# Eighteen instead of twenty seven-product tiles in the last feed-forward part, and attention products that lag one item more

## What is computed

```
def block(args):                      # forgetting attention, per block of 128 queries
    s = jnp.einsum('bhqd,bhkd->bhqk', q_i, kf) + c_i[..., :, None] - c[..., None, :]
    s = jnp.where(key_pos[None, :] <= q_pos[:, None], s, -jnp.inf)
    p = jax.nn.softmax(s, axis=-1)
    return jnp.einsum('bhqk,bhkd->bhqd', p, vf)
...
def swiglu(h, w1, w3, w2):            # w1, w3: 1024 x 2816, w2: 2816 x 1024
    return (jax.nn.silu(h @ w1) * (h @ w3)) @ w2
```

## Time and profile before

| what | us |
|---|---|
| median of 3 runs (lowest to highest) | 1707.92 (1707.61 to 1709.17) |
| the profiled execution, its own time | 1708.51 |
| its span, first to last instruction | 1706.7 |
| first block's attention, scores of item 0 to the last product with values | 259.3 to 362.5 |
| products of the twenty tiles, first to last | 1348.6 to 1564.7 |
| down products, first | 1568.25 |

### The profile page before, as it was taken

One profiled execution on the slowest core, in us unless ns is written; L12 is line 12 of the kernel. 1 busy time (PEld: TensorE's weight loads), 2 busy tenths in 40 slices (PEclk: granted clock), 3 DMA queues, 4 the chain that ended last, 5 costly groups with the idle time before them and its releaser, 6 DMA issues. The chain is left out here.

```text
span 1706.7 us, 21205 instructions
## 1 busy us (share of the span) xinstructions
PE 1595.5 (93%) x8576; PEld 1335.1 (78%) x8576; DVE 1056.9 (62%) x1458; ACT 700.4 (41%) x1021; POOL 439.5 (26%) x360
## 2 busy tenths in 40 slices
PE   5999988988999999999799999998899899998996
PEld 5778875766878888788788778887787899998885
DVE  6675547447987486433765543346853699998333
ACT  5644245543533243323632334444444544443222
POOL 0023303320622011100052012223432655553002
PEclk8999999989999899999899999999999999999998
DMA  7242212342254254222426423224443132224211
GB/s 285 99 148 75 75 62 89 118 176 99 99 173 164 107 197 173 99 99 74 147 99 248 130 76 109 85 84 152 151 166 124 38 112 99 99 100 148 76 73 50
DMA packets 46924, 203.93 MB, mean 119 GB/s; under 512 B 14337, under 2 KB 14721, under 8 KB 28203
## 3 DMA queue, kind: packets, MB, share of 16 engines
q1 hardware_dynamic: 37202, 171.84, 28.1%
q0 software_dynamic: 9088, 30.38, 5.3%
q10 hardware_dynamic: 536, 0.35, 0.1%
HBM read 181.56 MB, written 21.00 MB: 119 GB/s over the span
## 5 line engine op out<-in xcount | busy, mean ns | idle before, releaser
L540 PE MATMUL ps<-xh,whi 128*128 128x512 f32 (+1 forms) x1096 | 395.5, 361 | 10.8 <-DVE wlo L1742 5.3
L542 PE MATMUL ps<-xh,wlo 128*128 128x512 f32 (+1 forms) x1096 | 390.0, 356 | 0.0
L541 PE MATMUL ps<-xl,whi 128*128 128x512 f32 (+1 forms) x1096 | 388.2, 354 | 0.0
L1742 DVE TENSOR_TENSOR wlo<-raw,whi 128x2048 fp32r<-128x2048 f32 x93 | 233.3, 2509 | 138.3 <-ACT whi L1132 138.3
L1132 ACT ACTIVATE whi<-raw 128x2048 fp32r<-128x2048 f32 (+1 forms) x173 | 221.9, 1310 | 137.8 <-PE ps L542 52.1
L540 PEld LDWEIGHTS ps<-xh,whi 128*128 128x128 f32 x1096 | 208.8, 190 | 53.0 <-issue 11.6
L541 PEld LDWEIGHTS ps<-xl,whi 128*128 128x128 f32 x1096 | 209.2, 191 | 29.3
L542 PEld LDWEIGHTS ps<-xh,wlo 128*128 128x128 f32 x1096 | 207.9, 190 | 31.0
L540 PE MATMUL ps<-whi,xh 128*128 128x512 f32 x304 | 122.9, 404 | 8.3 <-ACT vr L1132 3.7
L542 PE MATMUL ps<-whi,xl 128*128 128x512 f32 x304 | 121.8, 401 | 0.0
L541 PE MATMUL ps<-wlo,xh 128*128 128x512 f32 x304 | 121.6, 400 | 0.0
(11 more groups left out here) (449 smaller groups left out, 3358.2 us busy)
## 6 DMA issues: line engine op xcount, KB each, us to landing
raw<-in_w_in SPq DMA_DIRECT2D x35, 1024.0 KB, 5.1
raw<-in_ffn_w SPq DMA_DIRECT2D x33, 1024.0 KB, 4.8
raw<-in_ada SPq DMA_DIRECT2D x24, 1024.0 KB, 4.8
raw<-in_w_up SPq DMA_DIRECT2D x22, 1024.0 KB, 4.8
raw<-in_w_down SPq DMA_DIRECT2D x11, 1024.0 KB, 4.8
xd<-X POOLq DMA_DIRECT2D x8, 512.0 KB, 6.1
td<-vr POOLq DMA_DIRECT2D x16, 256.0 KB, 3.6
raw<-td SPq DMA_DIRECT2D x4, 1024.0 KB, 5.3
```

What stands on the lines that cost most here:

```text
L540: pe.e.matmul(o, lh, rh, start=start, stop=False)
L541: pe.e.matmul(o, lh, rl, start=False, stop=False)
L542: return pe.e.matmul(o, ll, rh, start=False, stop=stop)
L1742: up(ve.e.tensor_tensor(lo, raw[conv_at[j] % 3][:, :], hi.bitcast(F32), ALU.subtract), "wlo")
```

## The change

Three things change in the last feed-forward part. Tiles 0 and 19 (`SLOW`) are done plainly again, with eight products (`whole_tile`): 96 matmuls of 256 columns where a fast tile has 84, four pieces (11, 21, 12, 22) where it has seven, no combinations on GpSimd, and no sums on VectorE; tile 0 goes from PSUM through ScalarE's silu, tile 19 from PSUM through VectorE's gate product. The ring has eight slots, `xrf` is free of it, ScalarE is seven pieces ahead and VectorE six. `xrf` holds the split half tokens of product 7 (`xs7`), which before were written over `xh4`/`xl4` late, so that `xh4`/`xl4` stay whole until tile 19; `dn2` moves to buffers that tile 18 uses last. The gate of the plain first pair comes after all token splits. In the first block's attention the products with the values lag four items: iteration i has `gather(i - 4)` and `scaled(i - 4)`, and both loops are one iteration longer.

```diff
+SLOW = (0, 19)
+FAST = [(n, p) for n in range(N_FAST) for p in ((11, 21, 12, 22) if n in SLOW else (1, 2, 5, 6, 3, 7, 4))]
...
+        xs7 = [xrf[:, 2:4, c:c + 512] for c in (512, 0)]
...
+        dn2 = [(x[:, 0:512], x[:, 512:1024]) for x in (flat(s2h), flat(s2l), xrf[:, 3, :], flat(cl)[:, 1024:2048])]
...
-            s = q % 10
+            s = slot(q)
...
-            for i in range(35):
+            for i in range(36):
...
-                if i >= 3:
-                    hd, t = divmod(i - 3, 4)
-                    gather(i - 3, pt1[(i - 3) % 3], [va[:, q, P * (hd // 2):P * (hd // 2) + P] for q in range(t + 1)])
+                if i >= 4:
+                    hd, t = divmod(i - 4, 4)
+                    gather(i - 4, pt1[(i - 4) % 3], [va[:, q, P * (hd // 2):P * (hd // 2) + P] for q in range(t + 1)])
...
+            def whole_tile(n, m):
+
+                p1, p2 = ((11, 21), (12, 22))[m]
+                b = take(("fast", n, p2), *(("f_a", FA["gated" if m else "gated21", n]) if n % 2 else
+                                            ("f_s", FS[f"silu{p2}", n])))
+                pe.wait_ge(sig["wlo"], item_no(n, p2))
+                for c in range(2):
+                    for k in range(8):
+                        h, l = place(FAST_AT[n, p2 if k // 4 else p1])
+                        o = mm3(b[:, 256 * c:256 * c + 256], h[:, k % 4, :], l[:, k % 4, :], half_tokens(xh4, k, c),
+                                half_tokens(xl4, k, c), k == 0, k == 7)
...
-                if q + 9 < len(FAST):
-                    fast_high(q + 9)
+                if q + 7 < len(FAST):
+                    fast_high(q + 7)
...
-                if q + 8 < len(FAST):
-                    fast_low(q + 8)
-                if q == 136:
+                if q + 6 < len(FAST):
+                    fast_low(q + 6)
+                if (n, p) == (N_FAST - 1, 21):
                     conv[0] = J_DOWN2
                     low_parts(J_DOWN2)
-                if q == 138:
-                    pieces(1, act2, dn2, only=range(4))
+                    for k in range(4):
+                        low_part(dn2[k][1], act2[:, k, :], dn2[k][0], "down1", k)
```

More of the change, by code:

```diff
@@ L212, with slot, last_of, before @@
 for _n, _p in FAST:
-    for _x in (["s1"] if _p == 2 else []) + (["silu"] if _p == 1 and _n % 2 else []):
+    for _x in (["s1"] if _p == 2 else []) + (["silu"] if _p in (1, 11) and _n % 2 and _n - 1 not in SLOW else []) \
+            + ([f"silu{_p}"] if _p in (21, 22) and _n % 2 == 0 else []):
         FS[_x, _n] = len(FS) + 3
-    for _x in {5: ["c11"], 6: ["u2"], 7: ["u34", "c22"], 4: ["c"] + ["gated"] * (_n % 2)}.get(_p, []):
+    for _x in {5: ["c11"], 6: ["u2"], 7: ["u34", "c22"], 4: ["c"] + ["gated"] * (_n % 2),
+               21: ["gated21"] * (_n % 2), 22: ["gated"] * (_n % 2)}.get(_p, []):
         FA[_x, _n] = len(FA) + 3
-TS = {x: 17 + i for i, x in enumerate((n, p) for n in range(N_FAST) for p in (5, 7, 6, 4))}
+TS = {x: 17 + i for i, x in enumerate((n, p) for n in range(N_FAST) if n not in SLOW for p in (5, 7, 6, 4))}
+def slot(q):
+    return (q - len(FAST)) % 8
+def last_of(n):
+    return 22 if n in SLOW else 4
+def before(n):
+    while n - 1 in SLOW:
+        n -= 1
+    return n - 1
 def item_no(n, p):
@@ L1423, in scalar_program, with pieces @@
                         channels(u)
-            def pieces(inst, src, dn, ready, first, begun=0, only=None):
+            def pieces(inst, src, dn, ready, first):
                 def one(k):
@@ L1438, in one @@
                     act(dn[k % 4][0][:, :], src[:, k, :], ACT.Copy, "sp_hi")
-                for k in only or range(begun, 4):
+                for k in range(4):
                     one(k)
-                for k in range(0 if only else NFF):
+                for k in range(NFF):
                     if k % 2 == 0:
@@ L2167, in vector_program, with pieces @@
                         channels(u)
-            def pieces(inst, src, dn, begun=0, only=None):
+            def pieces(inst, src, dn, begun=0):
                 def one(k):
                     low_part(dn[k % 4][1][:, :], src[:, k, :], dn[k % 4][0][:, :], f"down{inst}", k)
-                for k in only or range(begun, 4):
+                for k in range(begun, 4):
                     one(k)
-                for k in range(0 if only else NFF):
+                for k in range(NFF):
                     if k % 2 == 0:
@@ L2457, in vector_program @@
                 y = flat(act2)[:, 512 * v:512 * v + 1024] if n % 2 else yg
-                if p == 5:
+                if p in (21, 22) and n % 2:
+                    m = p - 21
+                    b = tile(("fast", n, p))
+                    ve.wait_ge(sig["f_s"], FS["silu", n] if n - 1 not in SLOW else FS[f"silu{p}", n - 1])
+                    up(ve.e.tensor_tensor(y[:, 512 * m:512 * m + 512], b[:, :], yg[:, 512 * m:512 * m + 512], ALU.mult),
+                       "f_a")
+                elif p == 5:
                     b = tile(("fast", n, 2))
-                    ve.wait_ge(sig["f_a"], FA["gated" if n % 2 == 0 else "c", n - 1] if n else 2)
+                    if n % 2 == 0:
+                        ve.wait_ge(sig["f_a"], FA["gated", n - 1] if n else 2)
                     ve.wait_ge(sig["f_s"], FS["s1", n])
```

120 lines of the change are left out of this document (61 added, 59 removed).

## The result

The changed kernel takes **1690.8 us** (median of 4 executions, 1689.2 to 1691.1) against 1708.6 of the kernel before on the same chip: a ratio of 0.9892, with a 95% interval of 0.9875 to 0.9909. It is faster by 17.7 us; 1692.1 was predicted, with a range of 1687 to 1702. The profiled execution took 1690.76, its span is 1689.0 (before: 1706.7), so the two traces differ by 17.7 as well.

What follows compares the result with a forecast made beforehand. TensorE, busy 93%, loses time only waiting or at low clock; VectorE sets 10.62 us a tile against its 10.08. Gains 2.4 + 4.8 + 2.1 + 1.5 + 1.0 + 4.0 = 15.8 give 1692.1 median, range 1687 to 1702.

Steps and rivals of the forecast that it cites:

- Attention: First attention, lag of four: 1.0 us gained at the start and 4.0 at the end, if the clock stays up.
- the 3.00: TensorE's wait of 3.00 us at 298.91 in the first attention, before a product with the values: claimed to stay.
- the 1.60: TensorE's wait of 1.60 us at 351.08, near the attention's end, with low clock behind it: claimed to go.
- rival A: Clock stays low at the end of the attention: 3.5 us less gain, 1695.6; chance 0.2.
- Tile 0: Start of the last feed-forward part: tile 1 starts at 1362.4, not 1364.79, 2.4 us gained (0.2 to 3.1).
- Tiles 1 to 18: Middle of the last feed-forward part: 4.8 us gained of 8.4 lost, a lead of about 4.0 shrinking 1.09 a pair.
- rival B: VectorE's pace bounds all the way: middle gives 0, shifted order may cost 0.5 a pair; 1697 to 1701.4; chance 0.14.
- Ring of eight: Shorter ring of pieces in the last feed-forward part: costs nothing, VectorE needing about 3 us against 7.2.
- Rival C: Shorter ring makes a closed loop, every odd tile stalls, nine tiles lose 2.0 us each: 1710.1; chance 0.03.
- Tile 19's end: Before the down products: the gap of 3.51 us goes, against 1.44 more of matmuls; 2.1 gained.
- the clock: At the first down products: without the gap the clock stays up, eight matmuls 0.235 apart, not 0.43; 1.5 us gained.
- D: Tiles gain but down products wait for w2's loads: price 3 us, 1695.1; chance 0.07.

Runs made afterwards that it cites:

- e11: Kernel before, its own leads, with GpSimd's subtractions cut from 512 columns to 32 in tiles 1 to 6 alone (output not the reference's): 1699.5 us, ratio 0.9942.
- e3: Kernel before with only the pieces' high and low parts made two products later (leads seven and six, were nine and eight): 1697.3 us, ratio 0.9925.
- e6: Changed kernel with ten memsets of 1024 columns put into VectorE's stream once, after the sums of product 60 (tile 8): 1697.0 us, ratio 0.9927.
- e5: Changed kernel with leads of six and five: 1691.0 us, ratio 0.9886.
- e9: Kernel before with later leads and the attention's lag of four, without the tiles of eight pieces and the new ring: 1690.7 us, ratio 0.9887.
- e12: Kernel before with the attention's lag of four and only VectorE's lower parts moved (six ahead), ScalarE's still nine ahead: 1692.3 us, ratio 0.9902.
- e8: Kernel before with GpSimd's four subtractions in each of tiles 1 to 19 cut from 512 columns to 32 (output not the reference's): 1696.6 us, ratio 0.9918.
- e10: Kernel before with the pieces' high and low parts made one product later (leads eight and seven): 1708.6 us, ratio 0.9988.
- e1: Kernel before with only the attention's part of the change, a lag of four items: 1704.4 us, ratio 0.9963.

## Why the prediction was right, and where it was not

The time was right by 1.3 us, the reasons in part; that it came so close is luck, as the last paragraph of this section works out.

- **Attention, 5.0 predicted.** At M the size is right: by eight profiles against six the lag is worth 5.2. At the start I wrote that the 3.00 would not go; it does, to 0.31 and 0.45, but the wait for GpSimd's `vr` before it grows from 1.24 (in before at 284.51) to 3.21, so much of it stands there instead, and the low clock with it. The net is 2.0 by the scores at 301.94 (303.95 in before), where I had 1.0. At the end the 1.60 goes as worked out, and further: I had the scores of item 31 at 349.5 to 351.5 and VectorE's largest score at 352.5; they came at 346.87 and 349.81, at the full clock, so rival A fell. New waits take part of it back (1.28 for `kr`, 2.24 for `pt`), and WO starts 5.7 earlier. What was missing: in the mean 7.3 are gained first and 2 given back by clock falls elsewhere.
- **Tile 0, 2.4 predicted.** Measured from M to tile 1's first product 37.9 against 40.1: 2.2. The wait for the second half was 0.61, I had 0.75.
- **Tiles 1 to 18, 4.8 predicted, 8.4 measured.** This is the step that failed: the term was mis-sized, because VectorE's pace was held fixed. I let VectorE keep its 21.25 a pair from the trace of before and gave tile 0's lead as the reason for the gain: a lead of 4 that shrinks by 1.09 a pair. e11 shows that this is how the old order behaves. But the change gives a new order, and there VectorE's pace is 19.45 without any lead (e3, e6), so no gap came in any pair. (A slip beside it: of the eight gaps of "0.86" the first, at 1405.60, is 0.36, for before had some lead too; the 8.4 lost stands, as it is counted from end to end.) I had considered the shifted order only in rival B, as a loss of 0.5 a pair. The bound of 8.4, no wait at all, was in the range.
- **Ring of eight, 0.** Nothing contradicts it, and there is room: even leads of six and five cost nothing (e5). Rival C, slower, did not come.
- **Tile 19's end, 2.1, and the clock, 1.5.** Both came as worked out. VectorE in after: the gate of the first half, w2's lower part, four down pieces, and then it waits for the second half.

```profile
1546.55 0.69 DVE L2497 TENSOR_TENSOR act<-ps,xr 128x512 f32<-128x512 f32 x1 [5.07 <-PE ps L559]
1547.15 2.28 DVE L1778 TENSOR_TENSOR wlo<-raw,whi 128x2048 fp32r<-128x2048 f32 x1
1549.35 1.29 DVE L1783 TENSOR_TENSOR s<-act,s 128x512 fp32r<-128x512 f32 x2
...
1551.16 0.69 DVE L1783 TENSOR_TENSOR clr<-act,clr 128x512 fp32r<-128x512 f32 x1
1552.31 0.69 DVE L2497 TENSOR_TENSOR act<-ps,xr 128x512 f32<-128x512 f32 x1 [0.46 <-PE ps L559]
```

  But I credited it to the shape of tile 19. With tiles of seven products, and VectorE not behind, the gap is 0.46 and the clock stays up as well (e3, e9, e12). So the old 3.51 was mostly VectorE's being behind.
- **D, w2's loads.** Did not appear: the first down product follows the last tile product directly.

**Luck in the sum.** It came close because two errors had opposite signs: the middle was 3.6 too small, and up to M this execution gained 3.4 where 5.0 stood. 15.8 + 3.6 - 1.6 - 0.2 (tile 0) = 17.6, of the 17.7 measured.

## What to carry to other kernels

When a change shifts an engine's instructions against another engine with which it contends, its pace of before is no longer known: bound it from below by the work it has without contention (here 14.9 us a pair, as e8 measured), do not take its pace of before for the upper bound without a reason, and take the mean ns of one instruction for a property of how the two streams meet, not of the instruction. If the pace is within some per cent of the bottleneck's, try the order's shift by itself first: here later leads and the longer lag alone (e9, 0.9887) gave what they gave together with a new ring, a new tile shape and new waits (0.9892). And read a gain that stands early in a trace again further on, in more than one profile, before you count it.

## What the runs showed of the hardware that I had not expected

- The same 14 lower parts, 10 sums and one gate product of a pair of tiles cost VectorE 14.9 us (GpSimd nearly idle), 16.7 (ahead of TensorE), 19.4 (behind, late leads) or 20.7 (behind, early leads) of busy time.
- Being ahead lowers an engine's own busy time, and the other's too: with VectorE waiting for TensorE part of the time GpSimd's eight subtractions take 11.8 a pair (after), against 13.1 with VectorE never waiting (e3). That they then run alone more often is my reading of it.
- Places one product apart (e10, and e3) differ by 1.7 us a pair; those of nine and eight and of eight and seven do not differ, but for one pair of e10 at 20.16.
- An early gain of 7.3 us arrives as 5.2 some 950 us later, with no code changed between: the low-clock stretches fall at other places (in after at about 430 and 480 us, where before has none). Executions of one kernel differ by up to 6 us in the same way (e1: 1701.3 at a mean clock of 0.980, 1707.3 at 0.974).
